# Two transformer blocks in fp32: the first layer's twelve narrow slabs take both halves of h at once, and modulation slabs move back

## Chip, cores and metric

The kernel runs on one core of one Trainium2 chip. The metric is the device time of one execution in microseconds. Before the change the median of three runs is 963.48 us (962.64 to 963.85).

## What is computed

256 tokens of width 1024 go through two models one after the other, all in float32. The first is one layer: a norm, a mixer (forgetting attention with 8 heads of 64, a gated convolution branch, two sigmoid gates, an output projection) and a gated network. The second has two layers, each with attention and a gated network, whose norms are scaled, shifted and gated by a modulation that is computed from a vector c.

```python
proj = h @ w_in                        # q, k, v, f_logit, g_b, g_c, hc, gate_conv, gate_attn
ya = g_b * causal_depthwise_conv(g_c * hc, conv_w)
yb = forgetting_attention(q, k, v, log_sigmoid(f_logit + b_f))
merged = sigmoid(gate_conv) * (ya @ w_branch[0]) + sigmoid(gate_attn) * (yb @ w_branch[1])
x = x + rmsnorm(merged @ w_out);  x = x + rmsnorm(swiglu(rmsnorm(x)))
...
mod = silu(c) @ ada_w[i] + ada_b[i]    # shift, scale and gain of both parts of layer i
h = rms_norm(x) * (1 + sc) + sh;  x = x + g * rms_norm(attention(h));  ...
```

## The kernel before

**Products in two halves.** float32 values are split into a high half (rounded) and a low half (the rest). A product is three matmuls: high weights by high values, high weights by low values, low weights by high values. The values h lie as `h_both`, for each chunk of 128 rows the high half of 256 tokens and then the low half.

**Slabs.** The weights come in 159 slabs of 128 x 2048 (1 MB), in the order of `slab_order` (line 61): 0 and 1 are the values of the first attention, 2 to 5 its queries and keys (qk1), 6 to 19 the mixer's other columns in the order mix 2, 4, 3, 5, 0, 1 (convolution branch) and mix 6 to 13 (gates), 20 to 23 the branch products, 24 to 27 the output projection, 28 to 60 the first network, 61 to 76 the second model's first attention, and so on. Between them `load_order` (line 92) puts the 48 modulation slabs. Its plan has, for each group, a count and the main slabs behind which the group's first and last stand, the others spread evenly between.

**Queues.** SP loads the stream of main and modulation slabs into 8 buffers in turn (`sp_load`, line 494): the load of an item waits until the item eight places before is used up, a main slab by TensorE's last matmul of it, a modulation slab by VectorE's sum. ScalarE rounds a main slab (`act_round`, line 502), VectorE takes the rest as the low half (`dve_rest`, line 509) and sums a modulation slab against c in two instructions (`dve_sum`, line 515). ScalarE and VectorE work through the items strictly in stream order, three main slabs ahead of the one that TensorE uses (`act_next` and `dve_next`, lines 550 and 555), and in between do what the current slab needs. Each engine's program is written out by hand, and each engine runs its own in order.

**Two ways to use a slab.** `pe_still` (line 569) waits for the low half of the slab, then does 48 matmuls of 256 columns, all sums in one PSUM bank; one engine reads the sum. `pe_both` (line 603) needs two banks: 16 matmuls of 512 columns put the high weights against both halves of h, and only then it waits for the slab's low half and adds 16 matmuls of 256 columns. `act_low` and `dve_low` (lines 631 and 638) add the bank's two halves: a copy by ScalarE of one, an addition by VectorE of the other. In the first layer `pe_still` is used for the four slabs of qk1, for mix 0 to 5 and for the first two gates, `pe_both` for the other six gates; the branch products are `pe_still` too. PSUM has 8 banks; without a number `bank` (line 284) takes banks 0 to 3 in turn, and waits until the owner's readers are done.

**Norms.** Between two stages stands a norm: `act_post_norm`, `dve_post_norm` and `pool_post_norm` (lines 386, 423 and 455), stage 0 behind the first layer's output projection, 1 behind the first network, 2 to 5 likewise in the second model. For each of two halves of the tokens VectorE multiplies by the gain, ScalarE squares, VectorE joins the sums (line 358), POOL takes the root (line 364), VectorE makes x (line 435), and after the same again scales x (line 369) for TensorE's transposes (line 320). VectorE comes to stage 0 only after the low halves of slabs 27, 28 and 29 (`wide`, line 1614), TensorE transposes the first half in the midst of the output projection (line 696). POOL also carries the modulation's gains from a column to rows by two DMAs (`pool_gain`, line 481).

**The start.** The first value slab is rounded, split and used in halves of 1024 columns; the second is waited for as a whole in `pe_moving` (line 657). Then come the queries and keys, the running sums of the gates (`ck`, line 1552), and heads of attention in steps between the mixer's slabs (`pe_attend1`, line 986).

Of the kernel before, what the change touches and what calls it, by code (L numbers as in the profile page):

```python
# [167 lines left out]
def build_program(nc, dram, out):  # L168
    with ExitStack() as ctx:
# [479 lines left out]
        def pe_moving(name, parts, data, ready, kcs, k_all, freed, tag, between={}):  # L649
# [336 lines left out]
        def pe_attend1(n):  # L986
# [163 lines left out]
        def gate_folded(n, g):  # L1150

            return n == 1 or g > 1


# [28 lines left out]
        def tensor():  # L1183
# [33 lines left out]
            def qk(g, keys):  # L1217
                yield from pe_still("qk1", 2 * keys + g, h_of, ready, [[(produced, ("k1", g)) if keys else (evacuated, ("q1", g))]])
# [18 lines left out]
            for g in range(2):  # L1237
                yield from pe_still("mix", 2 + g, h_of, ready, [[(evacuated, ("zc", g))]])
                yield from pe_attend1(2 * g + 2)
                yield from pe_still("mix", 4 + g, h_of, ready, [[(produced, ("z", g))]])  # L1240
                yield from pe_attend1(2 * g + 3)
            for g in range(2):
                yield from pe_still("mix", g, h_of, ready, [[(produced, ("conv", g))]])
                yield from pe_attend1(6 + g)
            for n in range(2):
                for g in range(4):
                    if gate_folded(n, g):
                        yield from pe_both("mix", 6 + 4 * n + g, ready, at=((4, 5) if g % 2 == 0 else (6, 7) if n else (None, None)))
                    else:
                        yield from pe_still("mix", 6 + 4 * n + g, h_of, ready, [[(evacuated, ("gate", n, g))]])  # L1250
# [67 lines left out]
        def scalar():  # L1318
# [34 lines left out]
            def query(g):  # L1353
                yield from act_next("qk1", g)
                yield from act.wait_ge(slab, ("qk1", g))
                yield from act.wait_ge(h_lo_made, ("in", 1, KC - 1))
                nc.scalar.activation(qT[:, 2 * g:2 * g + 2, :], pair(bank_of["qk1", g, 0]), ACT.Copy, scale=HD1 ** -0.5).then_inc(
                    *evacuated.up(("q1", g)))

            yield from query(0)  # L1360
            yield from act_next("qk1", 2)
# [448 lines left out]
```

## Time and profile before

| | |
|---|---|
| median of three runs | 963.48 us |
| the profiled execution | 962.54 us, of it the span 961.2 us |
| TensorE busy | 953.2 us (99%) |
| VectorE, ScalarE, POOL busy | 740.0, 544.8 and 34.2 us |
| HBM read | 223.49 MB, 234 GB/s over the span |

The page gives shares over the whole span. Matmuls overlap in the pipeline, so a group's busy time counts overlapping parts twice when groups are added; how long a slab takes is read from the starts of its first matmul and of what follows it. A small hole between matmuls does not show as idle time where the previous matmul's modelled end lies behind it.

### The profile page before, as it was taken

The page shows a single profiled execution, that of the slowest core. Times are in us where ns is not written, and L with a number is a line of the kernel's source. Part 1 is how long each engine was busy: PE and PEld are TensorE (multiplying, and loading weights), DVE is VectorE, ACT ScalarE, POOL GpSimd, SP SyncE. Part 2 cuts the span into 40 slices and gives each one's busy share as a digit, 9 for nine tenths or more (in the row PEclk, how much of TensorE's full clock was granted, in tenths as well). Part 3 has the DMA queues.
Part 4 walks back from the last instruction along what each step waited for, and adds up shares of the span by engine and source line. Part 5 has one row for each costly group of instructions (what it writes and reads, how often), then busy time and mean ns, then how long its engine had stood idle before and what let it go on. Part 6 is the DMA issues. An engine that isn't in the chain of part 4 may idle for free.

```text
span 961.2 us, 13438 instructions
## 1 busy us (share of the span) xinstructions
PE 953.2 (99%) x5418; PEld 827.7 (86%) x5418; DVE 740.0 (77%) x1145; ACT 544.8 (57%) x838; POOL 34.2 (4%) x58
## 2 busy tenths in 40 slices
PE   9999999999999999999999999999999999999997
PEld 7999989888888888888888888888888888888886
DVE  7799978788877767988678878766897678766563
ACT  6745553565455656665565454656776675454551
POOL 2000000020000001000000000001000100000000
PEclk9999999999999999999999999999999999999999
DMA  9877788498777753776467677763743266668511
GB/s 366 335 276 263 262 308 313 173 200 343 269 295 300 286 204 135 270 269 264 185 248 296 247 293 271 270 250 137 241 138 125 88 243 239 219 184 320 176 44 45
DMA packets 33151, 225.64 MB, mean 235 GB/s; under 512 B 4058, under 2 KB 4341, under 8 KB 6720
## 3 DMA queue, kind: packets, MB, share of 16 engines
q1 hardware_dynamic: 30960, 219.43, 61.8%
q0 software_dynamic: 1696, 5.08, 2.0%
q8 instruction: 43, 0.70, 0.3%
q10 hardware_dynamic: 432, 0.26, 0.1%
q14 instruction: 20, 0.16, 0.0%
HBM read 223.49 MB, written 1.26 MB: 234 GB/s over the span
## 4 chain that ended last, share of the span: by engine, by line
PE 93%; DVE 2%; DMA 2%; ACT 2%; SPq 0%; POOL 0%; issue 0%; DVEq 0%
PE psum L623 30%; PE psum L628 16%; PE psum L668 10%; PE psum L669 10%; PE psum L670 10%; PE psum L585 3%; PE psum L586 3%; PE psum L587 3%; DMA raw<-in_qk 2%; PE psum L888 2%; PE psum L740 1%; PE psum L739 1%; PE psum L741 1%; PE psum L320 1%; PE psum L956 1%; PE psum L601 0%
## 5 line engine op out<-in xcount | busy, mean ns | idle before, releaser
L512 DVE TENSOR_TENSOR low<-raw,high 128x2048 fp32r<-128x2048 f32 (+1 forms) x160 | 361.1, 2275 | 95.1 <-ACT high L506 95.0
L506 ACT ACTIVATE high<-raw 128x2048 fp32r<-128x2048 f32 (+1 forms) x160 | 299.9, 1897 | 15.1 <-DMA raw<-in_moba_qk 4.8
L623 PE MATMUL psum<-h_both,high 128*128 128x512 f32 x1272 | 305.3, 392 | 0.0
L623 PEld LDWEIGHTS psum<-h_both,high 128*128 128x128 f32 x1272 | 235.5, 188 | 48.2 <-issue 1.5
L628 PEld LDWEIGHTS psum<-h_both,low 128*128 128x128 f32 x1312 | 168.3, 191 | 6.4
L628 PE MATMUL psum<-h_both,low 128*128 128x256 f32 x1312 | 170.2, 283 | 0.0
L668 PE MATMUL psum<-high,y_hi 128*128 128x512 f32 x328 | 129.3, 394 | 0.0
L669 PE MATMUL psum<-low,y_hi 128*128 128x512 f32 x328 | 128.1, 391 | 0.0
L670 PE MATMUL psum<-high,y_lo 128*128 128x512 f32 x328 | 127.8, 390 | 0.0
L635 ACT ACTIVATE work_v<-psum 128x256 f32<-128x256 f32 x120 | 45.6, 383 | 142.2 <-PE psum L628 142.2
L521 DVE CUSTOM_DVE_ANT_0 raw<-raw,c_row 128x1024 f32<-128x1024 f32 x96 | 113.4, 1219 | 0.0
L670 PEld LDWEIGHTS psum<-high,y_lo 128*128 128x128 f32 x328 | 61.6, 188 | 13.1
L668 PEld LDWEIGHTS psum<-high,y_hi 128*128 128x128 f32 x328 | 61.7, 188 | 11.9 <-DVE y_lo L978 0.2
L669 PEld LDWEIGHTS psum<-low,y_hi 128*128 128x128 f32 x328 | 61.8, 188 | 11.4
L643 DVE TENSOR_TENSOR work_v<-psum,work_v 128x256 f32<-128x256 f32 x120 | 47.9, 420 | 23.4 <-ACT work_v L635 23.3
L585 PE MATMUL psum<-h_both,high 128*128 128x256 f32 x192 | 55.3, 288 | 0.0
L586 PE MATMUL psum<-h_both,high 128*128 128x256 f32 x192 | 54.4, 283 | 0.0
L587 PE MATMUL psum<-h_both,low 128*128 128x256 f32 x192 | 54.4, 283 | 0.0
L809 ACT ACTIVATE y_hi<-work_v 128x512 fp32r<-128x512 f32 x30 | 19.0, 632 | 48.4 <-DVE work_v L831 48.4
L668 PE MATMUL psum<-high,h_both 128*128 128x512 f32 x104 | 41.6, 400 | 0.1
L670 PE MATMUL psum<-high,h_both 128*128 128x512 f32 x104 | 40.6, 391 | 0.0
L669 PE MATMUL psum<-low,h_both 128*128 128x512 f32 x104 | 40.6, 390 | 0.0
(195 smaller groups left out, 1033.6 us busy)
## 6 DMA issues: line engine op xcount, KB each, us to landing
raw<-in_gate_up SPq DMA_DIRECT2D x66, 1024.0 KB, 5.5
raw<-in_ada SPq DMA_DIRECT2D x48, 1024.0 KB, 4.9
raw<-in_down SPq DMA_DIRECT2D x33, 1024.0 KB, 4.9
raw<-in_mix SPq DMA_DIRECT2D x14, 1024.0 KB, 6.9
raw<-in_moba_qk SPq DMA_DIRECT2D x8, 1024.0 KB, 5.2
raw<-in_diff_qk SPq DMA_DIRECT2D x8, 1024.0 KB, 4.9
raw<-in_qk SPq DMA_DIRECT2D x4, 1024.0 KB, 16.2
raw<-in_branch SPq DMA_DIRECT2D x4, 1024.0 KB, 6.3
```

Source lines behind the costliest of these rows:

```text
L506: nc.scalar.activation(high[n % N_HI][:, s], raw[i % N_RAW][:, s], ACT.Copy).then_inc(*rounded.up(n if key is None else key))
L512: nc.vector.tensor_tensor(low[i % N_RAW][:, s], raw[i % N_RAW][:, s], high[n % N_HI][:, s].bitcast(F32), ALU.subtract).then_inc(*rest.up(key))
L521: last = nc.vector.tensor_tensor_reduce(out=w, in0=w, in1=c_row[:, :], scale=1.0, scalar=0.0, op0=ALU.mult, op1=ALU.add, accum_out=mod_raw ...
L585: nc.tensor.matmul(to, a, hi(k), start=first, stop=False)
L586: nc.tensor.matmul(to, a, lo(k), start=False, stop=False)
L587: m = nc.tensor.matmul(to, r, hi(k), start=False, stop=last and j > j0)
L623: nc.tensor.matmul(o[:, :], a, h_both[:, k, :, :], start=k == 0, stop=False)
L628: m = nc.tensor.matmul(o[:, 0:S], wl[:, k, j * P:(j + 1) * P], h_hi[:, k, :], start=False, stop=k == KC - 1)
L643: m = nc.vector.tensor_tensor(place[:, j, :], o, place[:, j, :], ALU.add)
L668: nc.tensor.matmul(psum[b][:, :], hi(k0 + k, t), vh, start=first, stop=False)
L669: nc.tensor.matmul(psum[b][:, :], hi(k0 + k, t), vl, start=False, stop=False)
L670: m = nc.tensor.matmul(psum[b][:, :], lo(k0 + k, t), vh, start=False, stop=last)
```

## The change

Five things. The twelve slabs that used `pe_still` in the first layer (qk1, mix 0 to 7) use `pe_both`, with banks named where banks 4 to 7 are free; every place that read one bank now adds two halves first, so VectorE takes part in each, and the scores wait for the joined sums of q and k instead of the evacuations. Nine modulation slabs instead of fourteen stand in the first layer, the first behind slab 9 (before: 4), the last behind slab 27 (before: 22); the groups of the first network and of the second model's first network take fourteen and thirteen instead of eleven each and begin earlier. The second value slab is rounded and split in halves, and TensorE waits for the first half, then halfway for the second. POOL waits, before the gains' first DMA, until x is scaled.

```diff
-    plan = [(14, 4, 22), (11, nets[0][0] + 4, nets[0][0] + 24), (8, nets[0][1] + 4, nets[1][0] - 2),
-            (11, nets[1][0] + 3, nets[1][0] + 26), (4, nets[2][0] + 4, nets[2][0] + 16)]
+    plan = [(9, 9, 27), (14, nets[0][0] + 2, nets[0][0] + 24), (8, nets[0][1] + 4, nets[1][0] - 2),
+            (13, nets[1][0] + 2, nets[1][0] + 25), (4, nets[2][0] + 4, nets[2][0] + 16)]
...
-                    yield from pe.wait_ge(rest, n)
+                    yield from pe.wait_ge(rest, (1, "a") if n == 1 else n)
...
                 for k in range(kcs):
+                    if n == 1 and k == kcs // 2:
+                        yield from pe.wait_ge(rest, n)
...
-                yield from pe.wait_ge(evacuated, ("q1", h // 4))
-                yield from pe.wait_ge(produced, ("k1", h // 4))
+                yield from pe.wait_ge(joined, ("qk1", h // 4, h // 2 % 2), ("qk1", 2 + h // 4, h // 2 % 2))
...
-                yield from pe_still("qk1", 2 * keys + g, h_of, ready, [[(produced, ("k1", g)) if keys else (evacuated, ("q1", g))]])
+                yield from pe_both("qk1", 2 * keys + g, ready, at=(6, 7) if keys == 1 and g == 0 else (5, 6) if keys else (None, None))
...
-                yield from pe_still("mix", 2 + g, h_of, ready, [[(evacuated, ("zc", g))]])
+                yield from pe_both("mix", 2 + g, ready)
...
-                yield from pe_still("mix", 4 + g, h_of, ready, [[(produced, ("z", g))]])
+                yield from pe_both("mix", 4 + g, ready, at=(5, 6))
...
-                yield from pe_still("mix", g, h_of, ready, [[(produced, ("conv", g))]])
+                yield from pe_both("mix", g, ready, at=(None, None) if g else (4, 6))
...
-                    if gate_folded(n, g):
-                        yield from pe_both("mix", 6 + 4 * n + g, ready, at=((4, 5) if g % 2 == 0 else (6, 7) if n else (None, None)))
-                    else:
-                        yield from pe_still("mix", 6 + 4 * n + g, h_of, ready, [[(evacuated, ("gate", n, g))]])
+                    yield from pe_both("mix", 6 + 4 * n + g, ready, at=((4, 5) if g % 2 == 0 else (6, 7) if n else (None, None)))
...
+            for i, kind, m in act.items(1):
+                yield from act_round(1, 1, slice(0, SLAB // 2), (1, "a"))
+                yield from act_round(1, 1, slice(SLAB // 2, SLAB))
...
+                yield from act_low(("mix", 4 + g), ya[:, 2 * g:2 * g + 2, :])
...
+                yield from act.wait_ge(small_dve, ("tap", AC - 1, 2))
+                yield from act_low(("mix", g), zc[:, 2 * g:2 * g + 2, :])
...
+            for i, kind, m in dve.items(1):
+                yield from dve_rest(1, 1, slice(0, SLAB // 2), (1, "a"))
+                yield from dve_rest(1, 1, slice(SLAB // 2, SLAB))
...
-                yield from dve.wait_ge(slab, ("mix", 4 + g))
-                yield from dve.wait_ge(evacuated, ("zc", g))
-                nc.vector.tensor_tensor(zc[:, two, :], pair(bank_of["mix", 4 + g, 0]), zc[:, two, :], ALU.mult).then_inc(
-                    *produced.up(("z", g)))
+                yield from dve_low(("mix", 4 + g), ya[:, two, :])
+                yield from dve.wait_ge(joined, ("mix", 4 + g, 1))
+                nc.vector.tensor_tensor(zc[:, two, :], ya[:, two, :], zc[:, two, :], ALU.mult).then_inc(*produced.up(("z", g)))
...
+            yield from pool.wait_ge(scaled, (1, NT - 1, 1))
             yield from pool_gain(0, 1, 0)
...
+            yield from pool.wait_ge(scaled, (3, NT - 1, 1))
             yield from pool_gain(1, 0, 1)
...
+            yield from pool.wait_ge(scaled, (4, NT - 1, 1))
             yield from pool_gain(1, 1, 2)
```

## Rows read from the trace of the kernel before

**Rows 1.** The page: busy time, and the granted clock in 40 slices.
```profile
PE 953.2 (99%) x5418; PEld 827.7 (86%) x5418; DVE 740.0 (77%) x1145; ACT 544.8 (57%) x838; POOL 34.2 (4%) x58
...
PEclk9999999999999999999999999999999999999999
```

**Rows 2.** Busy time by stretch, 48 to 96 us: PE, PEld, DVE, ACT, POOL, clock.
```profile
48.00:96.00 48.00, 48.00 (x400) 45.85 (x399) 47.20 (x92) 24.78 (x50) 0.00 (x0) 1.00 0.72 271
```

**Rows 3.** Timeline of TensorE (start, length): mix 5 from its first matmul, what follows.
```profile
74.66 0.38 PE L585 MATMUL psum<-h_both,high 128*128 128x256 f32 x1
...
80.52 0.49 PE L956 MATMUL psum<-const,prob 128*128 128x128 f32 x3
```

**Rows 4.** Timeline of TensorE: mix 9, and the first matmuls of mix 10.
```profile
115.14 3.92 PE L623 MATMUL psum<-h_both,high 128*128 128x512 f32 x16
118.90 2.08 PE L628 MATMUL psum<-h_both,low 128*128 128x256 f32 x16
120.81 3.82 PE L623 MATMUL psum<-h_both,high 128*128 128x512 f32 x16
```

**Rows 5.** The page's groups (busy, mean ns, idle before): addition of halves, and rounding.
```profile
L643 DVE TENSOR_TENSOR work_v<-psum,work_v 128x256 f32<-128x256 f32 x120 | 47.9, 420 | 23.4 <-ACT work_v L635 23.3
...
L506 ACT ACTIVATE high<-raw 128x2048 fp32r<-128x2048 f32 (+1 forms) x160 | 299.9, 1897 | 15.1 <-DMA raw<-in_moba_qk 4.8
```

**Rows 6.** Timeline of VectorE: start of a modulation slab's sum, and what follows it.
```profile
33.83 1.21 DVE L521 CUSTOM_DVE_ANT_0 raw<-raw,c_row 128x1024 f32<-128x1024 f32 x1
...
36.12 2.29 DVE L512 TENSOR_TENSOR low<-raw,high 128x2048 fp32r<-128x2048 f32 x1
```

**Rows 7.** Timeline of TensorE: forget logits, then the second value slab.
```profile
17.05 2.03 PE L1205 MATMUL psum<-h_both,wf_both 128*16 128x512 f32 x8
19.21 0.50 PE L668 MATMUL psum<-high,h_both 128*128 128x512 f32 x1
```

**Rows 8.** Timeline of TensorE: the first scores (in brackets, idle time and releaser).
```profile
45.13 0.46 PE L888 MATMUL psum<-work 64*128 64x128 f32 x2 [0.42 <-DVE ck L1552]
```

**Rows 9.** Timeline of POOL: the gain's first DMA at stage 1.
```profile
378.54 1.05 POOL L486 DMA_DIRECT2D gain_dram<-gain_col  x1
```

**Rows 10.** Timeline of VectorE: scaling of the second half at stages 1 and 2.
```profile
378.62 1.19 DVE L369 TENSOR_SCALAR work<-x_res,stat 128x512 f32<-128x512 f32 x2 [0.66 <-POOL stat L364]
...
482.45 0.88 DVE L369 TENSOR_SCALAR work<-x_res,stat 128x512 f32<-128x512 f32 x2 [0.66 <-POOL stat L364]
```

**Rows 11.** Timeline of TensorE: the transposes behind them, stages 1 and 2.
```profile
379.26 1.27 PE L320 MATMUL psum<-const,work 128*128 128x128 f32 x8
...
483.09 1.06 PE L320 MATMUL psum<-const,work 128*128 128x128 f32 x8
```

**Rows 12.** Timeline of VectorE ahead of stage 0: three low halves, then the gain.
```profile
173.32 6.70 DVE L512 TENSOR_TENSOR low<-raw,high 128x2048 fp32r<-128x2048 f32 x3 [1.11 <-ACT high L506]
179.93 0.68 DVE L420 TENSOR_TENSOR work<-psum,gain 128x512 f32<-128x512 f32 x1
```

**Rows 13.** Timeline of ScalarE: the square beside it.
```profile
179.94 0.60 ACT L352 ACTIVATE work_v<-psum 128x512 f32<-128x512 f32 x1 [2.03 <-PE psum L670]
```

**Rows 14.** Timeline of TensorE: the first transposes of stage 0.
```profile
185.28 1.06 PE L320 MATMUL psum<-const,work 128*128 128x128 f32 x8
```

**Rows 15.** Timeline of VectorE: branch products 0 and 2 multiplied by their gates.
```profile
148.90 1.28 DVE L1603 TENSOR_TENSOR work<-psum,work 128x512 f32<-128x512 f32 x2
...
157.68 0.69 DVE L1603 TENSOR_TENSOR bias<-psum,bias 128x512 f32<-128x512 f32 x1 [1.58 <-PE psum L587]
```

**Rows 16.** Timeline of ScalarE: slab 25 rounded.
```profile
150.66 1.92 ACT L506 ACTIVATE high<-raw 128x2048 fp32r<-128x2048 f32 x1 [0.53 <-DMA raw<-in_out]
```

**Rows 17.** The page's DMA issues: KB each, median us from issue to landing.
```profile
raw<-in_ada SPq DMA_DIRECT2D x48, 1024.0 KB, 4.9
```

**Rows 18.** Timeline of VectorE: the turned rows' low half in the first network.
```profile
207.77 0.69 DVE L769 TENSOR_TENSOR y_lo<-psum,y_hi 128x512 fp32r<-128x512 f32 x1 [0.23 <-ACT y_hi L765]
```

**Rows 19.** Timeline of TensorE: the first matmul of the first down slab.
```profile
212.54 0.40 PE L668 MATMUL psum<-high,y_hi 128*128 128x512 f32 x1
```

More of the change, by code:

```diff
@@ L1354, in query, with key @@
                 yield from act_next("qk1", g)
-                yield from act.wait_ge(slab, ("qk1", g))
                 yield from act.wait_ge(h_lo_made, ("in", 1, KC - 1))
-                nc.scalar.activation(qT[:, 2 * g:2 * g + 2, :], pair(bank_of["qk1", g, 0]), ACT.Copy, scale=HD1 ** -0.5).then_inc(
-                    *evacuated.up(("q1", g)))
+                yield from act_low(("qk1", g), qT[:, 2 * g:2 * g + 2, :], HD1 ** -0.5)
+            def key(g):
+                yield from act_next("qk1", 2 + g)
+                yield from act_low(("qk1", 2 + g), kT[:, 2 * g:2 * g + 2, :])
             yield from query(0)
-            yield from act_next("qk1", 2)
+            yield from key(0)
             yield from act.wait_ge(small_dve, "cq")
@@ L1366, in scalar @@
             yield from act_attend1(0)
-            yield from act_next("qk1", 3)
+            yield from key(1)
             yield from act_attend1(1)
@@ L1370, in scalar @@
                 yield from act_next("mix", 2 + g)
-                yield from act.wait_ge(slab, ("mix", 2 + g))
-                nc.scalar.activation(zc[:, 2 * g:2 * g + 2, :], pair(bank_of["mix", 2 + g, 0]), ACT.Copy).then_inc(
-                    *evacuated.up(("zc", g)))
+                yield from act_low(("mix", 2 + g), zc[:, 2 * g:2 * g + 2, :])
                 yield from act_attend1(2 * g + 2)
                 yield from act_next("mix", 4 + g)
+                yield from act_low(("mix", 4 + g), ya[:, 2 * g:2 * g + 2, :])
                 yield from act_attend1(2 * g + 3)
@@ L1391, in scalar @@
                     two = slice(2 * g, 2 * g + 2)
-                    yield from act.wait_ge(lo_made, ("conv", 1))
-                    if gate_folded(n, g):
-                        yield from act_low(("mix", index), place[:, two, :])
-                        yield from act.wait_ge(joined, ("mix", index, 1))
-                        src = place[:, two, :]
-                    else:
-                        yield from act.wait_ge(slab, ("mix", index))
-                        src = pair(bank_of["mix", index, 0])
-                    nc.scalar.activation(place[:, two, :], src, ACT.Sigmoid).then_inc(*evacuated.up(("gate", n, g)))
+                    if n == 1:
+                        yield from act.wait_ge(lo_made, ("conv", 1))
+                    yield from act_low(("mix", index), place[:, two, :])
+                    yield from act.wait_ge(joined, ("mix", index, 1))
+                    nc.scalar.activation(place[:, two, :], place[:, two, :], ACT.Sigmoid).then_inc(*evacuated.up(("gate", n, g)))
                     if n == 0 and g < 3:
@@ L1541, in key @@
                 yield from dve_next("qk1", 2 + g)
-                yield from dve.wait_ge(slab, ("qk1", 2 + g))
-                nc.vector.tensor_copy(kT[:, 2 * g:2 * g + 2, :], pair(bank_of["qk1", 2 + g, 0])).then_inc(*produced.up(("k1", g)))
+                yield from dve_low(("qk1", 2 + g), kT[:, 2 * g:2 * g + 2, :])
             yield from dve_next("qk1", 0)
+            yield from dve_low(("qk1", 0), qT[:, 0:2, :], HD1 ** -0.5)
             yield from key(0)
@@ L1554, in vector @@
             yield from dve_next("qk1", 1)
+            yield from dve_low(("qk1", 1), qT[:, 2:4, :], HD1 ** -0.5)
             yield from dve_attend1(0)
@@ L1578, in vector @@
                 yield from dve_next("mix", g)
-                yield from dve.wait_ge(slab, ("mix", g))
+                yield from dve_low(("mix", g), zc[:, two, :])
+                yield from dve.wait_ge(joined, ("mix", g, 1))
                 yield from dve.wait_ge(small_dve, ("tap", AC - 1, 2))
-                nc.vector.tensor_tensor(ya[:, two, :], pair(bank_of["mix", g, 0]), ya[:, two, :], ALU.mult).then_inc(
-                    *produced.up(("conv", g)))
+                nc.vector.tensor_tensor(ya[:, two, :], zc[:, two, :], ya[:, two, :], ALU.mult).then_inc(*produced.up(("conv", g)))
                 yield from dve_attend1(6 + g)
@@ L1590, in vector @@
                     yield from dve_next("mix", index)
-                    if gate_folded(n, g):
-                        yield from dve_low(("mix", index), place[:, 2 * g:2 * g + 2, :])
+                    yield from dve_low(("mix", index), place[:, 2 * g:2 * g + 2, :])
                     if n == 0 and g < 3:
```

3 lines of the change are left out of this document (1 added, 2 removed).

## The prediction, made before the changed kernel ran

> **What bounds the kernel now.** Read the page first. TensorE is busy for 953.2 of 961.2 us, and its granted clock stands at the upper of its two levels, 2.4 GHz, in every slice [rows 1]. So a microsecond counts only if it shortens TensorE's own stream or a hole in it. VectorE is nearly full in the first layer, 47.2 of 48 us, but TensorE is full there too, with 48.00 [rows 2]: work taken off VectorE there gives nothing by itself. The timelines then give what a slab (1 MB of weights) costs on TensorE, and the places where another engine ends last. The sum is made against the profiled execution, 962.54 us with a span of 961.2; the median of the runs, 963.48, lies 0.9 above it, and what the sum gives is added to that. No change means within 0.2% (1.93 us), about what a measurement of this kernel can tell.
>
> **Twelve slabs in the wider form.** The four slabs of qk1, six of the convolution branch and the first two gates go from 48 matmuls of 256 columns to 16 of 512 and 16 of 256. The old form takes from 74.66 to 80.52, 5.86 us [rows 3]; the new one, between other work in the same way, from 115.14 to 120.81, 5.67 us [rows 4]. That is 0.19 us for a slab and 12 x 0.19 = **2.3 us** off TensorE's stream. Both forms stream 12,288 columns, so the far end is 0 (rival D).
> The Trainium skill, "TensorE: Matmul & The Clock Gate", section "Back-to-back issue gap", gives a warm matmul N/2.4 + 2.5 ns; by that alone 16 matmuls fewer are worth 0.04 us a slab, 0.5 us in all, and the sum below would come out at 965.6. The rows have this kernel's own shapes and show 0.19, so they are used.
>
> The two halves must now be added: a ScalarE copy and a VectorE addition for each of two banks, VectorE's part 420 ns each [rows 5], 12 x 0.84 = 10.1 us more on VectorE, less the copies that go. Against that five modulation slabs leave the first layer; one costs VectorE 36.12 - 33.83 = 2.3 us [rows 6], so 11.5 us. VectorE's load stays about where it is. The new waits for a bank's sum come a slab or more after the bank is full; the tightest (bank 6 for mix 0, filled by mix 5 just before) is asked for eight matmuls, 1.9 us, into mix 0, while the addition takes 0.4 and the copy about as long. I take 0 and bound it by 1. ScalarE's new wait for the last tap stands ahead of a copy that must wait for TensorE anyway.
>
> **The second slab in halves.** TensorE starts the forget logits at 17.05 and the second value slab at 19.21 [rows 7]. Eight matmuls of 512 columns at (118.90 - 115.14)/16 = 0.235 us [rows 4] would be through at 18.9, so 0.3 us is a wait for the low half, with all of TensorE's stream queued behind it. VectorE now makes the first half 1.1 us sooner: **0.3 us** (0 to 0.3). One more instruction on ScalarE and on VectorE is hidden behind the logits; without them it would cost some 0.1.
>
> **The first scores.** TensorE waits 0.42 us for ck [rows 8]. Ahead of ck VectorE sums two modulation slabs, the first from 33.83 [rows 6]. Both move behind slab 9: 4.6 us less, against 1.7 us of additions for two slabs. ck comes in time: **0.4 us** (0 to 0.4).
>
> **POOL waits until x is scaled.** After the first network (stage 1) POOL issues a DMA from 378.54 for 1.05 us [rows 9], and the two scalings beside it take 1.19 us; the same pair in the next norm, without a DMA beside it, takes 0.88 [rows 10]. The eight transposes behind it take 1.27 us instead of 1.06 [rows 11]. Stage 3 shows the same, so 2 x 0.21 = **0.4 us**. At stage 1 the DMA is gone, since its modulation slabs come later; at stage 3 it moves behind the scalings and meets the splitting of h, so 0.2 is the low end. Behind POOL's new wait stand that gain's DMA and the next norm's powers, a stage away: nobody waits.
>
> **Where it is given back: modulation slabs ahead of the first norm.** Before, none stood between slabs 22 and 32. Now the eighth stands behind slab 24 and the ninth behind slab 27, and VectorE takes slabs strictly in order. At the end of the output projection VectorE makes the low halves of slabs 27, 28 and 29 back to back from 173.32, and multiplies by the gain at once, at 179.93 [rows 12]; ScalarE squares the other half from 179.94 on, 0.60 us [rows 13]. Both join at 180.6, and nothing is spare. From there it is one chain (root, x, squares, scaling), and TensorE's transposes begin at 185.28 [rows 14]: no idle time stands in the row, so I allow 0.1 us in hand. The ninth slab's 2.3 us go in between slabs 27 and 28; the chain is **2.3 us** late, and TensorE, in order, stands.
> The eighth adds to it. It goes between the low halves of slabs 24 and 25, and with it the ring of 8 buffers moves on: slab 25 takes the buffer of slab 20, the first of the branch product, which TensorE reads until 148.9 (VectorE's multiplication of its sums starts at 148.90 [rows 15]); SP can issue the load only then. Before, slab 25 had landed by 150.66 [rows 16]. A load takes 4.9 us [rows 17], rounding 1.9 [rows 5], the low half 6.70/3 = 2.2 [rows 12], two multiplications 1.3 [rows 15]: 148.9 + 10.3 = 159.2, where the next multiplication began at 157.68, held by TensorE [rows 15]. That is 1.5 late; the merged halves, slab 26 and slab 27 follow on VectorE and ScalarE without a gap, so it arrives at 173.32 as well. Were the load there in time, VectorE alone would be 0.5 late. Total: 2.3 + 1.5 - 0.1 = **3.7 us** lost; bounds 2.2 (nothing from the eighth) and 4.7 (a load slower by 1 us).
>
> **Behind that.** In the first network modulation slabs now stand behind slabs 30 and 31, where the first stood behind 32: 4.6 us more on VectorE ahead of the turned rows' low half. ScalarE rounds slab 32 late anyway, so 3.2 of it arrives there: done at 208.5 [rows 18], it would be done at 211.7, and TensorE asks for it at 212.54 [rows 19]. 0.8 is in hand; I take 0. The second network gets one slab more ahead of the same step and is taken alike. The first layer's two gain DMAs come some 15 us later; loads beside them are slow, but were asked for four slabs, some 22 us, ahead.
>
> **Sum.** -2.3 - 0.3 - 0.4 - 0.4 + 3.7 = +0.3 us: 962.8 for the profiled execution, **963.8 us** for the median (963.48 + 0.3). With the terms at their far ends (gains 2.6 to 3.4, loss 2.2 to 4.7) this case reaches from 962.3 to 965.6.
>
> **Rivals.**
> A. *The hold at the first norm does not come*: VectorE gets the modulation slabs done earlier than I count. For it: VectorE waits 1.1 us for ScalarE right before 173.32 [rows 12]. Against it: the order is written out, and the ninth cannot pass slab 27. Then only the gains stay: 963.5 - 3.4 = 960.1, faster. Chance 0.22.
> B. *TensorE's clock falls in the hole.* 3.7 us is longer than any hole in the trace, and the granted clock never left 2.4 GHz [rows 1]. If it drops to 1.2 GHz for as long as the hole is, 3.7 us hold half the work, 1.8 us more: 965.6, slower. It decides whether other work breaks the hole. Chance 0.10. The Trainium skill, same page, section "The HAM clock gate", says that an array left idle returns to half its clock; no run here shows it yet.
> C. *VectorE is late in both networks*: the 0.8 us in hand is used up by one more low half, 2.2 us. TensorE then waits 1.4 us at the first down slab, twice: 966.6. It decides at the end of the turned rows' low half. Against it: everything there counts from TensorE's own stream. Chance 0.07.
> D. *Columns alone count*, and the change does not do what it says, as the wider form saves nothing: 963.8 + 2.3 = 966.1. Against it: [rows 3, 4]. Chance 0.05.
>
> **How the numbers follow.** The forecast has 0.56. Faster (below 961.5): A, and 0.03 of the forecast for terms beyond their bounds, 0.25. Slower (above 965.4): C, D, two thirds of B and 0.01 of the forecast, 0.20. Same: 0.55. The range reaches from A's value to D's, 960.0 to 966.1, and leaves out half of A and C, under 0.2; the likeliest case's own range is 962.3 to 965.6.
>
> **What would show it.** Slabs of 5.67 us in qk1 and the mixer; no wait for ck; the second value slab at 18.9; scalings of 0.88 at stages 1 and 3. The heart of it is a hole of 2 to 5 us in TensorE ahead of the first norm's transposes, with a modulation sum on VectorE between slabs 27 and 28. No hole there, or holes at bank waits in the mixer, would prove it wrong.

## The result, and the profile after

The changed kernel takes **967.58 us** (median of six runs, 965.34 to 968.40); the kernel before took 962.87 beside it (962.55 to 963.85). The ratio is 1.0044, 95% interval 1.0031 to 1.0057: slower by 0.4%. The forecast was no change, 963.8, with 966.1 as the upper end of its range; the median lies 1.5 us above that end.

The profiled execution is the fastest of the six: 965.34 us with a span of 964.0, 2.8 more than before, at full clock throughout. The other five lie 1.6 to 3.1 us above it, at mean granted clocks of 0.995 to 0.998. So there are two losses to explain: 2.8 us of waits, and some 2 us by which the median lies above the profiled execution, in runs with lower mean clocks. A mean clock of 0.998 alone does not prove a loss: the kernel before has a run of 962.47 us at 0.998 (beside experiment 10).

The first shows when the same matmul is looked for in both traces (starts on TensorE in us, from the timelines):

| on TensorE | before | after | difference |
|---|---|---|---|
| branch products begin | 143.07 | 139.92 | -3.15 |
| first norm's transposes (stage 0) | 185.28 | 186.85 | +1.57 |
| last slab of gate_up in the first network done | 356.26 | 357.83 | +1.57 |
| transposes of stage 1, first half | 369.98 | 373.18 | +3.20 |
| second model's first value slab | 380.28 | 383.29 | +3.01 |
| transposes of stage 3, first half | 658.59 | 661.58 | +2.99 |
| second attention's first value slab | 669.25 | 671.68 | +2.43 |
| transposes of stage 4, first half | 768.53 | 771.34 | +2.81 |
| last matmul | 955.71 | 958.50 | +2.79 |

The first layer brings 3.15 us up to the branch products. Then 4.72 are lost at the first norm, and 1.63 at the end of the first network. The page after, as in [rows 1]:

```profile
PE 950.9 (99%) x5226; PEld 817.3 (85%) x5226; DVE 743.6 (77%) x1168; ACT 542.3 (56%) x859; POOL 34.2 (4%) x58
...
PEclk9999999999999999999999999999999999999999
```

TensorE in the first layer, against [rows 3, 4, 7, 8] (start, length; in brackets idle time and releaser): the second value slab, the first scores, and mix 0 with what follows.

```profile
16.94 2.02 PE L1201 MATMUL psum<-h_both,wf_both 128*16 128x512 f32 x8
18.80 0.39 PE L670 MATMUL psum<-high,h_both 128*128 128x512 f32 x1
...
43.54 0.49 PE L890 MATMUL psum<-work 64*128 64x128 f32 x2
...
78.31 3.90 PE L623 MATMUL psum<-h_both,high 128*128 128x512 f32 x16
82.06 2.07 PE L628 MATMUL psum<-h_both,low 128*128 128x256 f32 x16
84.06 0.44 PE L997 MATMUL psum<-prob_t,work_v 128*64 128x256 f32 x2
```

Mix 0 takes 5.75 us (84.06 - 78.31) where it took 5.92 in the narrow form; the logits are followed at once by the second value slab; no wait stands before the scores. Now VectorE ahead of stage 0, as in [rows 12], and what TensorE waited for between 150 and 190 us (total, times, longest):

```profile
172.75 2.29 DVE L512 TENSOR_TENSOR low<-raw,high 128x2048 fp32r<-128x2048 f32 x1 [1.11 <-ACT high L506]
174.96 1.22 DVE L521 CUSTOM_DVE_ANT_0 raw<-raw,c_row 128x1024 f32<-128x1024 f32 x1
...
177.25 4.49 DVE L512 TENSOR_TENSOR low<-raw,high 128x2048 fp32r<-128x2048 f32 x2
181.65 0.69 DVE L420 TENSOR_TENSOR work<-psum,gain 128x512 f32<-128x512 f32 x1
```

```profile
PE psum L320 <- DVE work L369: 3.3, 1, 3.3
PE psum L670 <- DVE low L512: 1.1, 1, 1.1
```

The modulation sum stands between the low halves of slabs 27 and 28, as forecast. But slab 27's low half itself is already 2.6 us late (172.75 against 173.32 - 3.15), and so TensorE waits twice, for that low half and for the scaled x. Between matmul starts the two waits are 1.23 and 3.47 us longer than a matmul's usual distance.

The end of the first network, where nothing was forecast. TensorE in its last down slab; VectorE's additions for the last gate slab, after and then before:

```profile
357.83 0.40 PE L670 MATMUL psum<-high,y_hi 128*128 128x512 f32 x1
...
364.80 0.47 PE L670 MATMUL psum<-high,y_hi 128*128 128x512 f32 x1 [1.34 <-DVE y_lo L837]
```

```profile
361.79 0.75 DVE L643 TENSOR_TENSOR work_v<-psum,work_v 128x256 f32<-128x256 f32 x2
...
363.96 0.69 DVE L837 TENSOR_TENSOR y_lo<-work_v,y_hi 128x512 fp32r<-128x512 f32 x1 [0.70 <-ACT y_hi L811]
```

```profile
357.07 0.75 DVE L643 TENSOR_TENSOR work_v<-psum,work_v 128x256 f32<-128x256 f32 x2
...
359.24 0.69 DVE L835 TENSOR_TENSOR y_lo<-work_v,y_hi 128x512 fp32r<-128x512 f32 x1 [0.70 <-ACT y_hi L809]
```

TensorE is done with that slab at 357.83 (before 356.26); the additions end at 362.54 (before 357.82). I call this distance VectorE's **lag**: 4.7 us after, 1.6 before. Traced back through the network it rises to 9.7 us at the fourth pair of gates (before: never over 3.2, and 1.0 to 1.1 from 256 us to the last pair).

### The profile page after: what moved, and what is told of

Same layout as the page of the kernel before. It is cut to its first block, busy times and chain, and to the rows that moved or that the text cites. A ratio compares the mean times of both kernels' runs of the same rounds, so it can differ in the third digit from the quotient of the medians.

```text
span 964.0 us, 13098 instructions
## 1 busy us (share of the span) xinstructions
PE 950.9 (99%) x5226; PEld 817.3 (85%) x5226; DVE 743.6 (77%) x1168; ACT 542.3 (56%) x859; POOL 34.2 (4%) x58
## 4 chain that ended last, share of the span: by engine, by line
PE 70%; DVE 20%; ACT 6%; DMA 2%; issue 1%; POOL 0%; DVEq 0%; ACTq 0%
PE psum L623 24%; PE psum L628 13%; DVE low L512 10%; PE psum L670 8%; PE psum L671 8%; PE psum L672 8%; ACT high L506 4%; DVE raw L521 3%; DMA raw<-in_gate_up 2%; PE psum L890 1%; PE psum L320 1%; PE psum L742 1%; PE psum L741 1%; PE psum L743 1%; DVE work_v L643 1%
## 5 line engine op out<-in xcount | busy, mean ns | idle before, releaser
L623 PE MATMUL psum<-h_both,high 128*128 128x512 f32 x1464 | 352.0, 392 | 0.0
L623 PEld LDWEIGHTS psum<-h_both,high 128*128 128x128 f32 x1464 | 270.5, 188 | 56.2 <-issue 2.4
L628 PEld LDWEIGHTS psum<-h_both,low 128*128 128x128 f32 x1504 | 192.8, 191 | 7.3
L628 PE MATMUL psum<-h_both,low 128*128 128x256 f32 x1504 | 195.1, 283 | 0.0
L635 ACT ACTIVATE work_v<-psum 128x256 f32<-128x256 f32 x120 | 42.5, 376 | 76.9 <-PE psum L628 76.7
L803 ACT ACTIVATE work_v<-work_v 128x512 f32<-128x512 f32 x30 | 19.0, 633 | 79.9 <-DVE work_v L643 79.9
L364 POOL TENSOR_TENSOR stat<-stat,minus_half 128x1 f32<-128x1 f32 x24 | 13.3, 555 | 681.3 <-DVE stat L358 681.3
L837 DVE TENSOR_TENSOR y_lo<-work_v,y_hi 128x512 fp32r<-128x512 f32 x30 | 20.8, 693 | 21.0 <-ACT y_hi L811 21.0
```

Of the source, the lines that this page charges most:

```text
L623: nc.tensor.matmul(o[:, :], a, h_both[:, k, :, :], start=k == 0, stop=False)
L628: m = nc.tensor.matmul(o[:, 0:S], wl[:, k, j * P:(j + 1) * P], h_hi[:, k, :], start=False, stop=k == KC - 1)
L635: nc.scalar.activation(place[:, j, :], psum[bank_of[*key, j]][:, S:2 * S], ACT.Copy, scale=scale).then_inc(*evacuated.up(("low", *key, j)))
L803: nc.scalar.activation(ffn_tmp(g)[:, 0], ffn_tmp(g)[:, 0], ACT.Silu).then_inc(*evacuated.up(("silu", f, g)))
L837: nc.vector.tensor_tensor(y_lo[:, s, :], ffn_tmp(g)[:, 1], y_hi[:, s, :].bitcast(F32), ALU.subtract).then_inc(*lo_made.up(("hidden", f, g)))
```

## The experiments

Most are one or two edits to the changed kernel. The fifth is one edit to the kernel before; the seventh and eighth change the form of several slabs and the plan together. Ratios are against the kernel before, run beside them.

**1. The first group ends at slab 22.**

```diff
-    plan = [(9, 9, 27), ...
+    plan = [(9, 9, 22), ...
```

> The changed kernel with one number altered: the first layer's nine modulation slabs end behind slab 22 instead of 27. Theory P (the positions behind slabs 24 and 27 make the hole): TensorE's two waits ahead of the first norm's transposes, 1.23 and 3.47 us, go; the 1.5 us wait in the last down slab of the first network stays, because that group is not touched. The profiled execution comes to 965.34 - 4.7 = 960.6. Theory C (the clock falls in the 3.5 us hole, which makes five of the six timed runs 1.6 to 3.1 us longer than the profiled one, at a mean clock of 0.995 to 0.998): without the hole all runs show clock 1.000 and lie within 1.3 us, median 960.5 to 961.5. Rival V (VectorE is late at the first norm because of the two-half additions, wherever the modulation slabs stand): at least 2 us of the hole stay, or appear in the mixer: 963 or more. Rival S (the spread has nothing to do with the hole): the runs still lie up to 3 us apart.

Measured: 964.71 us (963.92 to 968.13), ratio 1.0016 (1.0008 to 1.0025); eleven of twelve runs within 1.4 us, at 0.999 or 1.000. Of the 4.7 us at the first norm 1.2 stay, and a new wait of 1.17 us between matmul starts stands in an attention step. TensorE's waits, 150 to 190 and 100 to 116 us:

```profile
PE psum L320 <- DVE work L369: 1.0, 1, 1.0
...
PE psum L997 <- ACT prob_t L966: 1.0, 1, 1.0
```

So both theory P and rival V hold in part. Where the 1.2 comes from is seen on VectorE and ScalarE at the end of the mixer, in the wide gates:

```profile
140.43 0.75 DVE L643 TENSOR_TENSOR bias<-psum,bias 128x256 f32<-128x256 f32 x2
143.68 2.29 DVE L512 TENSOR_TENSOR low<-raw,high 128x2048 fp32r<-128x2048 f32 x1 [2.50 <-ACT high L506]
145.89 0.75 DVE L643 TENSOR_TENSOR bias<-psum,bias 128x256 f32<-128x256 f32 x2
```

```profile
141.21 0.63 ACT L1395 ACTIVATE bias<-bias 128x512 f32<-128x512 f32 x1 [2.58 <-DVE bias L643]
141.75 1.90 ACT L506 ACTIVATE high<-raw 128x2048 fp32r<-128x2048 f32 x1
...
146.68 0.63 ACT L1395 ACTIVATE bias<-bias 128x512 f32<-128x512 f32 x1 [2.48 <-DVE bias L643]
```

Each engine shows 2.5 us of idle time a slab, and still neither has any to give: ScalarE's sigmoid waits for VectorE's addition, its next rounding follows the sigmoid, VectorE's low half waits for that rounding, and the next addition follows it. Once round takes 145.89 - 140.43 = 5.46 us, and TensorE's slab 5.57. A delay shrinks by 0.1 us a slab, and a modulation sum (2.3) lengthens it at once.

**2. The first network's group as before, three modulation slabs in the second attention. 3. Both edits.**

```diff
-            (14, nets[0][0] + 2, nets[0][0] + 24), ... (4, ...
+            (11, nets[0][0] + 4, nets[0][0] + 24), ... (3, nets[1][1] + 4, nets[1][1] + 10), (4, ...
```

> The changed kernel with the first network's group put back to eleven modulation slabs, from the fourth to the twenty-fourth slab of the network, as before; the three that are over go into the second model's second attention, behind its slabs 4 to 10. Theory L (fourteen modulation slabs make VectorE late all through the first network, 4.7 us still at its end against 1.6 before, which shows as the 1.5 us wait in its last down slab): that wait goes, the lag at the end is 1 to 2 us; the hole ahead of the first norm stays at 4.7. Profiled execution with clock 1.000: 965.34 - 1.5 = 963.8; median 967.58 - 1.5 = 966.1, because the clock still falls in the hole that stays. Rival K (the lag comes from the late start at the first norm, not from the count): the wait in the last down slab stays, 965.3 and 967.6. Rival for the clock (it falls in the later, 1.5 us wait): all runs at 1.000, median 963.8.

> Both edits together: the first group ends behind slab 22, the first network's group is eleven as before, three modulation slabs go into the second model's second attention. Theories P and L: both holes are gone and nothing takes their place, 965.34 - 4.7 - 1.5 = 959.1 profiled, all clocks 1.000, median 959.0 to 960.0: faster than the kernel before (962.9) by 3 to 4 us. Rival: three more sums in the second attention make VectorE late there or at the norm behind it, 1 to 2 us, 960 to 961.5. Rival V as above: 962 or more.

Measured: 973.13 (ratio 1.0103, 1.0090 to 1.0116) and 971.30 (1.0084, 1.0071 to 1.0097). In both the wait in the first network is gone and the lag at its end 1.6 us, as theory L says; but the three slabs cost more where they went. In experiment 2 TensorE waits in the second attention, and in the first one's output projection:

```profile
PE psum L1101 <- DVE work L645: 1.9, 1, 1.9
PE psum L958 <- DVE prob L949: 1.3, 1, 1.3
...
PE psum L670 <- DVE work L643: 1.2, 1, 1.2
```

The last one comes with POOL's second column DMA, which now starts at 416.91 instead of 396.59; that the one makes the other was not tried. The medians were missed by 7 and 11 us.

**4. The plan of before with the rest of the change.**

> The changed kernel with the whole plan of before: fourteen modulation slabs in the first layer behind slabs 4 to 22, eleven in each of the first two networks. The wider form, the halves of the second slab and POOL's waits stay. Theory M (the plan was moved because VectorE has no room for both): VectorE had 0.8 us idle in 48 to 96 us before, the additions are 10.1 us more, so it falls behind in the mixer, TensorE waits there for sums or low halves, 3 to 9 us in all, and the wait for ck comes back (0.4): profiled 962 to 968. Rival F (VectorE has room, since most of its busy time was there only because it could run ahead): no holes, 962.54 - 3.3 - 0.6 = 958.6, and the move of the plan brought nothing but losses.

Measured: 967.84 (967.61 to 968.91), ratio 1.0048 (1.0035 to 1.0061). Theory M: the old plan and the wide form together leave VectorE no room. TensorE's waits between 40 and 90 us:

```profile
PE psum L623 <- DVE bias L643: 2.6, 1, 2.6
PE psum L890 <- DVE ck L1550: 2.5, 1, 2.5
```

The 1.17 us at the first norm stand here too, with no modulation slab behind slab 22.

**5. The new plan alone, in the kernel before.**

> The kernel before with nothing but the new plan: nine modulation slabs in the first layer behind slabs 9 to 27, fourteen and thirteen in the two networks; the narrow form, the undivided second slab and POOL's early DMAs stay. Theory A (the holes add: 3.5 us of the 4.7 ahead of the first norm come from the positions behind slabs 24 and 27, 1.2 from VectorE and ScalarE leaving the mixer late because of the wider form): a hole of 3.0 to 3.7 us ahead of the first norm's transposes, 1.5 us in the last down slab of the first network, the wait for ck gone (-0.4): profiled 966.5 to 967.3, and the clock falls in some runs, so the median may lie 1 to 2 above that. Rival W (without the wider form VectorE has the room, and the positions alone cost nothing at the norm): 962 to 964. Rival N (the first network's hole needs the late first norm of the changed kernel's wider form): none there.

Measured: 968.33 (966.33 to 970.01), ratio 1.0046 (1.0028 to 1.0064). Theory A: 3.47 us at the first norm, in one wait, and 1.23 in the last down slab. The plan alone costs as much as the whole change. Here the profiled execution has the fallen clock (busy time by stretch, as in [rows 2]):

```profile
184.50:188.00 3.50, 0.25 (x2) 0.00 (x0) 1.97 (x5) 1.96 (x6) 0.55 (x1) 1.00 0.55 201
...
189.00:190.00 1.00, 1.00 (x6) 0.77 (x5) 0.58 (x2) 1.00 (x6) 0.00 (x0) 0.62 0.99 418
190.00:191.00 1.00, 1.00 (x4) 0.80 (x3) 0.83 (x4) 0.90 (x4) 0.00 (x0) 0.50 1.01 426
191.00:192.00 1.00, 1.00 (x4) 0.81 (x3) 0.96 (x2) 0.00 (x0) 0.00 (x0) 0.50 0.30 123
192.00:193.00 1.00, 1.00 (x4) 0.76 (x4) 0.09 (x1) 0.00 (x0) 0.00 (x0) 0.67 0.00 0
```

TensorE stands in the hole (0.25 of 3.5 us), does its transposes, and then runs at 1.2 GHz, matmuls of 512 columns 0.43 us apart instead of 0.23, until about 192.6. The twelve matmuls behind the transposes take 4.41 us instead of 2.83: 1.6 us for one fall. The one run at clock 1.000 took 966.33, the other five 1.6 to 3.7 more. Five profiles of this study have the 3.5 us hole unfilled, and the fall stands right behind it in four (experiments 2, 5, 9 and 11), where the transposes and these twelve matmuls take 5.2 to 5.3 us; in the fifth, the changed kernel's own, without a fall, 3.65.

**6. The ninth modulation slab moved to the second network.**

```diff
-    plan = [(9, 9, 27), (14, ...), ... (13, ...
+    plan = [(8, 9, 24), (14, ...), ... (14, ...
```

> The changed kernel with the ninth modulation slab, behind slab 27, moved to the second network (first group eight, behind slabs 9 to 24; second network fourteen). Theory A (the ninth is one sum of 2.3 us in VectorE's chain ahead of the first norm, the eighth 1.3, the late exit from the mixer 1.2): of 4.7 us 2.3 to 2.5 stay; the 1.5 in the first network stays; the second network has one more, its lag at the end grows from 2.0 to 3 us, without a hole. Profiled 965.34 - 2.3 = 963.0; the clock falls less often, median 963 to 964.5. Rival X (the eighth's load alone makes the hole, the ninth sum lies beside TensorE's work): 4 us or more stay, 965.

Measured: 965.83 (965.09 to 970.71), ratio 1.0026 (1.0014 to 1.0038). At the first norm 1.45 + 1.15 = 2.6 us are left of 4.7, and a new wait of 0.5 stands at 161 us: from the first branch product to the first norm's transposes it takes 3.2 us longer than before (45.44 against 42.21 us), so 1.5 came back without the ninth. That is not the ninth's price alone, because three other modulation slabs moved by a place as well. Two things came otherwise: the 1.5 us in the first network were gone (lag 2.4 at its end, with the same fourteen slabs in the same places, but POOL's column DMA at 232.65 instead of 223.71), and fourteen in the second network made a wait of 1.03 in its last down slab. The first led to experiment 9.

**7. Wide form in qk1 alone.** The narrow form is back in the convolution branch and both gates; the second slab in halves and POOL's waits stay.

```diff
-    plan = [(9, 9, 27), (14, nets[0][0] + 2, nets[0][0] + 24), ...
+    plan = [(12, 6, 22), (11, nets[0][0] + 4, nets[0][0] + 24), ...
```

> A version meant to be faster than both: the wider form only in the four slabs of qk1, where VectorE is idle; the convolution branch and the first two gates in the narrow form as before; the second slab in halves; POOL's waits; twelve modulation slabs in the first layer behind slabs 6 to 22, eleven in the first network as before, thirteen in the second. Theory A (what hurts is VectorE's and ScalarE's chain in the mixer and the network, not the wider form in itself): 4 x 0.19 = 0.8 from qk1, 0.3 from the second slab, 0.4 from ck, 0.7 from POOL's waits, no hole at the first norm or in the networks: 962.54 - 2.2 = 960.3 profiled, median 960.5 to 961.5. Rival B (two more modulation slabs around slabs 6 to 8 make VectorE late in the mixer): holes of 1 to 3 us there, 961.5 to 963.5.

Measured: **960.32** (960.27 to 962.02), ratio 0.9968 (0.9956 to 0.9979): faster than both kernels, as theory A says, and TensorE's waits show nothing between 30 and 700 us. The profiled execution happens to be the slowest of the eight, with 0.9 us lost at 25 us and 0.5 at 777.

**8. Narrow gates, ten slabs behind 7 to 22, eleven and fifteen in the networks.**

> The changed kernel with the first two gates back in the narrow form, ten modulation slabs in the first layer behind slabs 7 to 22, eleven in the first network as before, fifteen in the second. Theory A (each wider slab adds a step to the chain ScalarE-VectorE-ScalarE, and a gate in the wide form leaves that chain no room to catch up): two narrow gates give the chain back 2 to 3 us, the exit from the mixer is in time, and the first norm's hole is under 0.5; fifteen in the second network leave it 3 to 4.5 us late at its end, a hole of 0 to 1.3 there. 962.54 - 10 x 0.19 - 0.3 - 0.4 - 0.7 + 0 to 1.3 = 959.2 to 960.5 profiled. Rival B: the six wide slabs of the convolution branch and ten modulation slabs are too much for VectorE between 50 and 110 us, holes of 1 to 4 us in the mixer, 960.5 to 963.5.

Measured: 964.68 (964.26 to 968.04), ratio 1.0014 (1.0004 to 1.0024). The first norm is in time. But 0.9 us are lost in the convolution branch, 0.9 in the second network's last down slab, and over 2 in the second model's first attention, where POOL's second column came late (402.39). Expected were 959.2 to 963.5.

**9. POOL's first gain behind the first network's norm.**

```diff
-            yield from pool_gain(0, 0, None)
             yield from pool_post_norm(1)
             yield from pool.wait_ge(scaled, (1, NT - 1, 1))
+            yield from pool_gain(0, 0, None)
             yield from pool_gain(0, 1, 0)
```

> The changed kernel with POOL's first gain (its column DMA stands at 223.71 in the changed kernel's trace, in the midst of the first network) moved behind the first network's norm. Theory D (the 1.5 us wait in the last down slab of the first network has two sources: three more modulation slabs, and the column DMA beside which the loads asked for between 225 and 247 us take 11 to 17 us instead of 5 to 8, so that ScalarE rounds slab 39 about 2 us late): VectorE's lag at the end of the network falls from 4.7 to about 2.7 us and the wait goes below 0.3; the hole ahead of the first norm stays at 4.7. Profiled with clock 1.000: 965.34 - 1.4 = 963.9, if the two columns behind one another do not hold up the loads of the second model's first attention; if they do, 0.5 to 2 us come back there, 964.5 to 966. Rival L (the count of fourteen alone makes the lag): 4.7 us of lag and the 1.5 us wait stay, 965.3. Median 1 to 2.5 above the profile, because the clock still falls.

Measured: 971.67 (970.50 to 972.45), ratio 1.0086 (1.0073 to 1.0099). In the first network theory D holds: the lag at its end is 2.7 and the wait is gone. In the changed kernel POOL's column DMA and ScalarE's rounding of slab 39 stand so (in brackets what ended the idle time), and behind them the time from issue to landing of the nine loads issued between 219 and 250 us, there and in this experiment:

```profile
223.71 0.91 POOL L486 DMA_DIRECT2D gain_dram<-gain_col  x1 [23.99 <-DVE gain_col L479]
234.32 0.58 POOL L490 DMA_DIRECT2D gain<-gain_dram  x1 [9.69 <-DMA gain_dram<-gain_col]
...
245.63 1.92 ACT L506 ACTIVATE high<-raw 128x2048 fp32r<-128x2048 f32 x1 [4.55 <-DMA raw<-in_gate_up]
```

```profile
DMA to landing us min/median/max: 4.8/12.8/17.1
```

```profile
DMA to landing us min/median/max: 4.6/5.3/7.0
```

But the two columns, now one behind the other (384.13 and 397.12), hold up the loads of the attention, and with the granted clock at 0.50 from 416 to 423 us this costs more than it gave:

```profile
412.11 1.91 ACT L506 ACTIVATE high<-raw 128x2048 fp32r<-128x2048 f32 x1 [10.85 <-DMA raw<-in_moba_qk]
```

```profile
416.82 0.77 PE L623 MATMUL psum<-h_both,high 128*128 128x512 f32 x1 [3.52 <-DVE work L645]
```

**10. The hole filled.** In `pe_turn`, ahead of the first transposes of stage 0, into the bank that they overwrite:

```diff
+                for i in range(14 if (stage, t, g) == (0, 0, 0) else 0):
+                    nc.tensor.matmul(o[:, :], y_hi[:, 0, 0:P], y_hi[:, 0:2, :], start=True, stop=True)
```

> The changed kernel with 14 matmuls of 512 columns more, put where TensorE waits ahead of the first norm's transposes: 14 x 0.228 = 3.2 us of work whose result is overwritten, in the 3.5 us hole. Nothing else is touched. Theory C (the clock falls because TensorE stands still there): with the hole filled all runs show clock 0.999 or 1.000, they lie within 1.5 us, and the median comes down to the changed kernel's profiled time, 965.3 to 966.0. Rival S (the longer runs have another cause): median 967.6 and clocks of 0.995 to 0.998 as without the matmuls. Rival T (the matmuls lie on the path, because the hole is shorter in most runs): 967 to 969 at clock 1.000.

Measured: 965.60 (965.21 to 969.21), ratio 1.0036 (1.0024 to 1.0049). Five of nine runs lie at 965.2 to 965.6, where one of six did (experiments 5 and 11, whose hole is as long, have one such short run of six each); four are still at 967.7 to 969.2 (mean clocks 0.997 to 0.999). TensorE is busy in the stretch of the hole:

```profile
183.10:186.60 3.50, 3.48 (x16) 2.55 (x15) 1.97 (x5) 1.96 (x6) 0.55 (x1) 1.00 0.68 211
```

With fourteen matmuls *more* the median is 2 us *less*. The intervals of the two ratios overlap, so this supports theory C and does not settle it alone; with the four traces that show the fall behind the hole I hold it for the cause of most of the difference between the changed kernel's profile and its median; that is argued, since no long run of the changed kernel has a trace. The four long runs speak for rival S in part.

What can lengthen a run without the hole is seen in experiments 6 and 12, whose profiles are long runs themselves (968.14 us, 3.1 above the shortest of that kernel, and 963.21, 3.4 above). The load of slab 3 lands at 21.5 and 21.1 us instead of 18.7, VectorE copies the forget logits that much later, and TensorE waits 1.8 and 1.6 us longer than usual. Then the clock falls, and the first 16 matmuls of the first query slab take 5.4 us instead of 3.75. In experiment 12 (TensorE, and a stretch as in [rows 2]):

```profile
25.98 0.38 PE L1213 MATMUL psum<-cols,work 16*128 16x8 f32 x2 [1.46 <-DVE work L1521]
```

```profile
28.00:29.00 1.00, 1.00 (x4) 0.80 (x3) 1.00 (x1) 1.00 (x1) 0.00 (x0) 0.50 1.02 426
```

So the start of the kernel is a second place where a run can lose 3 us. Which of the two places lengthened the five long runs of the changed kernel is open.

**11. Without POOL's waits.** The three lines that wait for `scaled` are taken out.

> The changed kernel without POOL's three waits until x is scaled. Theory Q (POOL's DMA issue beside VectorE's scaling stretches it, and the transposes behind it): only stage 3 is left, since the first gains come elsewhere than at a scaling in the new plan at stage 1; scalings at stage 3 take 1.2 instead of 0.88 us and TensorE waits 0.5 us more ahead of their transposes: 0.3 to 0.6 slower at the second model's first norm behind the network, 965.6 to 965.9 profiled at clock 1.000. Rival Z (the waits do nothing): the same to 0.1.

Measured: 967.10 (965.59 to 969.79), ratio 1.0041 (1.0027 to 1.0055): within the spread of the changed kernel. At stage 3 a scaling lies beside POOL's DMA again (first VectorE, then POOL):

```profile
672.41 1.19 DVE L369 TENSOR_SCALAR work<-x_res,stat 128x512 f32<-128x512 f32 x2 [0.67 <-POOL stat L364]
```

```profile
672.33 1.05 POOL L486 DMA_DIRECT2D gain_dram<-gain_col  x1
```

The transposes behind it take 0.2 us more. At stage 1 nothing changes.

**12. Experiment 1 with narrow gates.**

> The first experiment (nine modulation slabs behind slabs 9 to 22) with the first two gates back in the narrow form. Theory A (a gate in the wide form is a chain of ScalarE's rounding, VectorE's low half, the additions and the sigmoid, 5.46 us against TensorE's 5.57, so a delay is not made up before the branch products; a narrow gate leaves out the copy and the addition in it): the 1.17 us wait of the attention step at 112 us and the 1.17 us ahead of the first norm go; 2 x 0.19 are lost; the wait in the last down slab of the first network, 1.7, stays: 964.62 - 2.3 + 0.4 = 962.7. Rival B (the six slabs of the convolution branch set the delay): both waits stay at over 0.8, 964.5 to 965.

Measured: **960.57** (959.86 to 963.56), ratio 0.9982 (0.9972 to 0.9991): theory A. Both waits of 1.17 us are gone, and the wait in the last down slab is down to 0.5. The last addition ends 1.0 us behind the mixer's last matmul, where experiment 1 had 4.5 (VectorE's addition and TensorE's first branch product):

```profile
143.72 0.85 DVE L643 TENSOR_TENSOR bias<-psum,bias 128x256 f32<-128x256 f32 x2
```

```profile
143.54 0.28 PE L585 MATMUL psum<-y_hi,high 128*128 128x256 f32 x1
```

## Why the prediction failed, step by step

The forecast had +0.3 us, and the median rose by 4.7 (962.87 to 967.58). Of the 4.4 between, 1.0 is the term of the first norm (3.7 in the sum, 4.7 measured), 1.6 the first network (0 in the sum), and some 1.9 the long runs (0 in the sum); the gains came out 0.1 better.

- **The twelve slabs, the second slab, ck** (2.3, 0.3 and 0.4): right. 3.15 us up to the branch products are 0.30 from the second slab (18.80 - 16.94 against 19.21 - 17.05), 0.42 from ck, 0.11 that the start came earlier, and 2.3 left for the slabs. No bank wait shows (the 1 us that the prediction allowed for one was missing from its range). Rival D falls.
- **POOL's waits** (0.4): right. Stage 1 gives 0.19 by the plan, since no gain falls there any more, as the prediction said; the wait itself does nothing there (experiment 11). Stage 3 gives 0.2 by the wait.
- **The first norm** (3.7, bounds 2.2 to 4.7): the mechanism right, the size 4.7. In the changed kernel's trace slab 27's low half is 2.6 us late, and the ninth slab's sum behind it adds 2.3 (forecast 2.3). Of the 2.6, experiment 1 leaves 1.2 without a modulation slab there, so the eighth is 1.4 (forecast 1.5); experiment 6 parts them less cleanly. Missing are the 1.2 us, from the step "VectorE's load stays about where it is". That step added up busy time over the first layer; what counts is the round that ScalarE and VectorE make together, which leaves a wide gate 0.1 us a slab to catch up. With the first two gates narrow these 1.2 are gone (experiment 12).
- **"Behind that"** (0): this step failed, by 1.63 us. It looked at the first down slab alone, where indeed no wait came. But the lag grows behind it and is not worked off before the last down slab, where TensorE waits. What failed is its sentence that the loads beside the gain DMAs were asked for early enough: loads beside the first column took up to 17 us, and slab 39, asked for at 230.9, held ScalarE up at 245.6. With that column out of the network (experiment 9), or 9 us later (experiment 6), the same fourteen slabs make no wait; eleven slabs with the column in the network make none either (experiments 2, 3 and 8). In these runs it takes both.
- **Rival B**, the clock, was given 0.10 because the trace of before had no such hole, which says nothing either way. That trace does show one fall, at its very end: the granted clock is 0.50 from 960 us on, 4 us after the last matmul. The mechanism exists and its 1.8 us were a fair price: one fall measures 1.6 us. Even so 965.6 was too low, since the waits alone came to 2.8 instead of 0.3. Forecast and rival are no alternatives: a case with a hole of 3.7 us had to carry B in its own price. The Trainium skill, "TensorE: Matmul & The Clock Gate", section "The HAM clock gate", says that the clock halves when the array goes idle; the 0.50 in experiment 5 agrees, while the changed kernel's profile shows that it need not come: its 3.47 us hole left the clock at 1.00.
- Rival A, that VectorE would be early, was wrong. Rival C had the right engine at the wrong end of the network.
- Not foreseen, and without effect: in nearly every trace one join of a norm comes 0.35 us later behind ScalarE's square than the others. Before it stood at stage 3, in the changed kernel at stage 4: 0.36 won at the one, 0.38 lost at the other. Its cause is open.

Added up, -3.15 + 4.72 + 1.63 - 0.19 - 0.2 - 0.36 + 0.38 = 2.8 us for the profiled execution; the median lies some 2 us higher, by the clock that falls at the norm, or by the waits and the clock at the start; which of them in which run is not shown.

## What to carry to other kernels

Idle time of two engines that wait for each other once a tile is not room: time the round they make, compare it with the bound engine's tile, and price added work by how fast a delay is worked off, down to the end of the loop. When a change is expected to open a hole of several us on TensorE, add the price of a fallen clock to the forecast itself. A better form of work for the bound engine is worth having where its helpers can work off the delay that it makes: four wide slabs (experiment 7) bring 0.3%, and ten wide slabs with the first group ending at slab 22 (experiment 12) 0.2%, with shortest runs of 960.27 and 959.86. What costs 0.4% here is not the wide form by itself: the new plan in the kernel before costs 0.5% (experiment 5).

## What was not expected of the hardware

- A hole costs more than its length: the fall of the clock behind one of 3.5 us took 1.6 us more. It does not follow every hole. In experiment 4 a wait of 2.7 us at 43 us left the clock at 1.00, and one as long at 83 us was followed by half the clock.
- A 4 KB column written to memory element by element held up 1 MB loads for over 20 us: those issued from 225 to 247 us took 11 to 17 us, where experiment 9 has 5 to 7. While the column was under way, 223.7 to 234.1 us, all queues together moved 30 GB/s, and 364 GB/s in the 9.8 us behind it. The Trainium skill, "DMA: Bandwidth & Descriptors", section "Rules for kernel authors", says that a last dimension that is not contiguous becomes one descriptor per element. This trace does not show it: for the column's 1024 values it has 32 packets beside SP's queue in that stretch.
